# A two-layer hybrid block on one core: the triangular levels of both directions' last delta-rule chunks take an earlier rank in the order of steps

## The chip, the cores and the metric

The kernel runs on one core of a Trainium2 chip. The metric is the device time of one execution in microseconds (us); lower is better. The time before is the median of three executions, 2316.86 us.

## The reference, cut to what matters

Two layers work on one sequence of 1024 tokens with 1024 features, in float32. The first has a windowed attention beside a bidirectional gated delta rule, an output projection of both, and a feed-forward part; the second has three other branches and plays no role here. The delta rule in chunks, and what the first layer makes of it:

```python
def _chunk_gated_delta_rule(q, k, v, g, beta):
    ...
    t_mat = lax.linalg.triangular_solve(eye + a_mat, jnp.broadcast_to(eye, a_mat.shape),
                                        left_side=True, lower=True)
    w_c = jnp.einsum("bnhcs,bnhsd->bnhcd", t_mat, beta[..., None] * k * jnp.exp(gc)[..., None])
    u_c = jnp.einsum("bnhcs,bnhse->bnhce", t_mat, beta[..., None] * v)
    ...
    def step(state, xs):
        q_c, k_c, u, w, qk_c, gl = xs
        v_new = u - jnp.einsum("bhcd,bhde->bhce", w, state)
        o = jnp.einsum("bhcd,bhde->bhce", q_c, state) + jnp.einsum("bhcs,bhse->bhce", qk_c, v_new)
        state = state * jnp.exp(gl)[..., None, None] + jnp.einsum("bhcd,bhce->bhde", k_c, v_new)
        return state, o

def _gdn_mixer(qkv, z, a, b, conv_w, a_log, dt_bias, norm_w):
    ...
    o_fwd = _chunk_gated_delta_rule(q, k, v, g[:, :, 0], beta[:, :, 0])
    o_bwd = flip(_chunk_gated_delta_rule(flip(q), flip(k), flip(v), flip(g[:, :, 1]), flip(beta[:, :, 1])))
    o = _rmsnorm(o_fwd + o_bwd, norm_w) * jax.nn.silu(z.astype(f32).reshape(B, S, GDN_HEADS, GDN_HEAD_DIM))

def first_block(...):
    ...
    h = h + jnp.concatenate([attn, gdn], axis=-1) @ w_out[l]
```

## The kernel before, in words

Large products run in three passes on TensorE (PE). A float32 operand is split into a high part, rounded to the format fp32r, and the rest, its low part; per slab of 128 input features PE multiplies high by high (line 625), low weight by high (627) and high by low (629). So each 128 x 512 result tile, a job, takes 24 matmuls over 8 slabs. The stage of these jobs after the delta rule is the output projection, called P3 in the code: jobs 46 to 61. Jobs 46 and 47 cover half 1 of the sequence, 48 and 49 half 0. In each, slabs 0 to 3 read attention, slabs 4 to 7 the normed and gated delta-rule output.

**The delta rule.** It runs in chunks of 128 tokens, i = 0 to 7, in two directions, d = 0 (forwards) and d = 1 (backwards). The inverse of each chunk's triangular matrix is built from 32 x 32 blocks in two levels, l = 0 and 1. A level is a line of small steps: `la` (PE, lines 747 and 754) multiplies, `lp` (VectorE, called DVE; 1544 and 1547) copies the result to the tile P, `lb` (PE, 747 and 754) multiplies again, `lt` (DVE, 1558 and 1562) subtracts it from the tile T, `lx` (PE, 734) transposes T, and `ltt` (ScalarE, called ACT; 991) copies that to TT. The `la`, `lb` and `lx` steps of all chunks share a ring of three PSUM banks.

**The recurrence.** With the inverse at hand, a chunk does `cR` (PE, 702) and `cr` (DVE, 1570), `cT` (PE, 702) and `cn` (ACT, 991), `co` (PE, 800 and 801) and `cO` (DVE, 1584). All but the last chunk also do `crk` (ACT), `ckd` (PE, 702) and `cs` (DVE, 1592) for the state. Of these, `cR`, `cT`, `co` and `ckd` share a ring of two banks with `gs`. The norm of a finished chunk is `gsq` (ACT, 1181), the sum over features `gs` (PE, 811), `gr` (ACT, 995 and 997) and `gn` (DVE, 1602).

**Attention.** It runs over 8 blocks n of 128 queries: `aqk` (PE, 822), `am` (DVE, 1614), `as1` (DVE, 1621 to 1624), `ae` (ACT, 1193), `as2` (DVE, 1629 and 1631), `ap` (GpSimd, called POOL; 2128), and per key block s `atr` (PE, 830), `atc` (ACT, 991) and `apv` (PE, 840); the result is copied out by `ao` (DVE, 1642).

**The operands of P3.** For each half h and each slab j of attention, `ya` (a DMA issued by SP) loads the stored result, `yah` (ACT) makes the high part and `yal` (DVE, 1419) the low part. For the delta rule, `zl` loads the gate, `zm` (DVE, 1653) multiplies it in once the `gn` of four chunks are done (those of direction 0, `gn(0, 4..7)`, for half 1; those of direction 1 for half 0), `zh` (ACT) makes the high part and `zlo` (POOL, 2083) the low part. Half 0 reuses the buffers of half 1, so `ya(0, j)` waits for `yal(1, j)`. Result tiles are added by `evd` (DVE, 1668); `hac` (1408 and 1410) sums squares, and `ws` (1779 to 1792) prepares weights for a later stage.

**The order of the work.** A planner, `Plan.settle`, places every step once, ahead of time, on its engine. It keeps one clock for each engine, made from estimated durations, and at each point takes the step that can start first. Among steps of an engine that can start at the same moment, the one with the lower rank goes first:

```python
t = start(q, k)
c = (max(t, clock[q] + 40), info[k][3], seq[k], k)
...
clock[q] = t + r.ns
ends[k] = clock[q] + self.LAG[q]
```

The order that comes out is fixed in the program: each engine runs its steps in that order and waits on semaphores for those of others. Steps of the triangular levels have rank r = 4 + i/8, attention steps 1.5 + n/16, steps of the recurrence 2, norm sums 3 (2 for chunk 7), and the parts of the P3 jobs 9. The names to follow are `first_layer` (the loop over i and d, where `la` to `ltt` are added), `Plan.settle`, and the steps above.

Of the kernel before, what the change touches and what calls it, by code (L numbers as in the profile page):

```python
# [181 lines left out]
class Plan:  # L182
# [15 lines left out]
    def add(self, engine, name, *key, rank=5, ring=None, frees=None, behind=()):  # L198


        self.steps.append((engine, name, key, rank, ring, frees, behind))
# [2680 lines left out]
def first_layer(p, K):  # L2882
# [70 lines left out]
    for i in range(8):  # L2953
        for d in range(2):
            r = 4 + i / 8
            add("sp", "inv_in", d, i, rank=r)
            add("pool", "tex", d, i, rank=r - 1)
            add("sp", "gcl", d, i, rank=r)
            add("sp", "bel", d, i, rank=r)
            add("dve", "dd", d, i, rank=r)  # L2960
            add("act", "ebx", d, i, rank=r)
            add("pool", "sc", d, i, rank=r)
            add("dve", "a1", d, i, rank=r)
            before = [("lx", (d, i - 2, TOP))] if i >= 2 else [("lb", (0, 0, TOP)), ("lb", (1, 0, TOP))] if i else []
            add("sp", "kkl", d, i, rank=r)
            add("dve", "a2", d, i, rank=r)
            if i < 4:
                add("pe", "qk", d, i, rank=r, ring="prep", frees=[("qkc", (d, i))], behind=before)
                add("act", "qkc", d, i, rank=r)
                add("sp", "qk_out", d, i, rank=r)  # L2970
            else:
                add("sp", "qk_in", d, i, rank=r)
            add("dve", "qkm", d, i, rank=r)
            for l in range(len(LEVELS)):
                add("pe", "la", d, i, l, rank=r, ring="prep", frees=[("lp", (d, i, l))])
                add("dve", "lp", d, i, l, rank=r)
                add("pe", "lb", d, i, l, rank=r, ring="prep", frees=[("lt", (d, i, l))])
                add("dve", "lt", d, i, l, rank=r)
                add("pe", "lx", d, i, l, rank=r, ring="prep", frees=[("ltt", (d, i, l))])
                add("act", "ltt", d, i, l, rank=r)  # L2980
            if i:
                add("pe", "cR", d, i, rank=2, ring="chain", frees=[("cr", (d, i))], behind=[("co", (d, i - 1))])
                add("dve", "cr", d, i, rank=2)
            add("pe", "cT", d, i, rank=2, ring="chain", frees=[("cn", (d, i))] + ([("crk", (d, i))] if i < 7 else []))
            add("act", "cn", d, i, rank=2)
            add("pe", "co", d, i, rank=2, ring="chain", frees=[("cO", (d, i))], behind=[("co", (1 - d, 7 - i))] if i >= 4 else ())
            add("dve", "cO", d, i, rank=2)
            if i < 7:
                add("act", "crk", d, i, rank=2)
                add("pe", "ckd", d, i, rank=2, ring="chain", frees=[("cs", (d, i))], behind=[("co", (d, i))])  # L2990
                add("dve", "cs", d, i, rank=2)
            if i >= 4:
                r = 3 if i < 7 else 2
                add("act", "gsq", d, i, rank=r)
                add("pe", "gs", d, i, rank=r, ring="chain", frees=[("gr", (d, i))])
                add("act", "gr", d, i, rank=r)
                add("dve", "gn", d, i, rank=r)
    for g in range(2):
        add("sp", "abias", g)
    for n in range(8):  # L3000
        r = 1.5 + n / 16
# [207 lines left out]
def build(nc, A, out):  # L3209
# [12 lines left out]
    for b, j in enumerate(B.jobs):  # L3222
# [14 lines left out]
        else:  # L3237
            p.add("dve", "evd", b, rank=1)
    first_layer(p, K)
    second_layer(p, K)  # L3240

# [151 lines left out]
```

## Time and profile before

| | |
|---|---|
| time of three executions | 2317.94, 2316.86, 2314.18 us; median 2316.86 |
| the profiled execution | 2318.24 us, its span 2316.1 us |
| granted TensorE clock over the span | 0.991 of full speed |
| busy share of the span | PE 97%, DVE 69%, ACT 48%, POOL 45% |
| chain that ended last, by engine | PE 86%, DVE 7%, issue 3%, ACT 2%, DMA 2%, POOL 1% |

The busy shares are means over the whole span. A row of a timeline has the start, the time that the instructions of the row covered, engine, line, operation, shapes and count, and in brackets how long the engine had been idle ahead of it and what released it. Float32 matmuls that are not of the three-pass kind show as two records each, so a `gs` is x2, and an `apv`, which has two matmuls, x4. A fast record of the three-pass kind lasts 0.39 us, but the next one starts 0.23 us after it.

### The profile page before, as it was taken

Reading aid. Unit: us, or ns where it says so; the run is one execution under the profiler, and the core shown is the slowest. Engines: PE = TensorE matmul, PEld = TensorE weight load, DVE = VectorE, ACT = ScalarE, POOL = GpSimd, SP = SyncE. Lnnn points to the kernel's source line nnn. Section 1 sums busy time; section 2 is a strip of 40 time slices with the busy share of each in tenths; the row PEclk is TensorE's granted clock in tenths of the full one; section 3 lists DMA queues with packets and bytes.
Section 4 is the critical chain, followed back from the end, with each engine's and each line's share of the span. In section 5 each row is a group of like instructions: output and inputs, shape, how many; then the busy total and the mean of one; then the engine's idle time right before and its main releaser. Section 6 shows DMA issues by size and latency. Waiting matters only on the chain.

```text
span 2316.1 us, 31264 instructions
## 1 busy us (share of the span) xinstructions
PE 2256.4 (97%) x11389; PEld 1785.5 (77%) x11389; DVE 1606.4 (69%) x2217; ACT 1111.2 (48%) x2008; POOL 1034.5 (45%) x643
## 2 busy tenths in 40 slices
PE   9999979898989999999999999999999999999999
PEld 6778867666868888887887777777788888888886
DVE  7865767766497555589548779878978665546745
ACT  5654155765255555544445455555623332225653
POOL 2212244444147666656866311111123775546763
PEclk9999989999999999999999999999999999999999
DMA  4113453325224444755452301111033333338654
GB/s 158 45 38 98 131 169 97 107 86 190 91 83 173 169 154 150 272 187 175 154 171 79 132 28 46 46 46 46 28 105 123 132 132 112 114 126 291 195 172 147
DMA packets 153764, 289.43 MB, mean 125 GB/s; under 512 B 34915, under 2 KB 44387, under 8 KB 153612
## 3 DMA queue, kind: packets, MB, share of 16 engines
q1 hardware_dynamic: 153612, 287.44, 37.2%
q8 instruction: 91, 1.49, 0.3%
q14 instruction: 61, 0.50, 0.1%
HBM read 207.88 MB, written 79.51 MB: 124 GB/s over the span
## 4 chain that ended last, share of the span: by engine, by line
PE 86%; DVE 7%; issue 3%; ACT 2%; DMA 2%; POOL 1%; SPq 0%; DVEq 0%; ACTq 0%; POOLq 0%
PE bank L625 12%; PE bank L629 12%; PE bank L857 12%; PE bank L855 12%; PE bank L853 12%; PE bank L627 12%; PE bank L702 2%; PE bank L918 2%; PE bank L949 2%; PE bank L931 1%; ACT t L991 1%; DVE t L1419 1%; PE bank L840 1%; PE bank L830 1%; DVE t L1410 1%
## 5 line engine op out<-in xcount | busy, mean ns | idle before, releaser
L2083 POOL TENSOR_TENSOR t<-t,t 128x512 fp32r<-128x512 f32 (+1 forms) x494 | 814.7, 1661 | 1078.5 <-ACT t L991 1075.3
L991 ACT ACTIVATE t<-t 128x512 fp32r<-128x512 f32 (+1 forms) x689 | 448.9, 676 | 665.9 <-PE bank L857 252.9
L625 PE MATMUL bank<-t,t 128*128 128x512 f32 x1360 | 550.0, 404 | 0.6 <-ACT t L991 0.6
L629 PE MATMUL bank<-t,t 128*128 128x512 f32 x1360 | 532.7, 392 | 3.2 <-DVE t L1419 2.7
L627 PE MATMUL bank<-t,t 128*128 128x512 f32 x1360 | 531.1, 391 | 1.5 <-POOL t L2083 1.5
L853 PE MATMUL bank<-t,t 128*128 128x512 f32 x1316 | 513.8, 390 | 9.9 <-DVE t L1803 8.3
L857 PE MATMUL bank<-t,t 128*128 128x512 f32 x1316 | 513.0, 390 | 1.5 <-DVE t L1419 1.5
L855 PE MATMUL bank<-t,t 128*128 128x512 f32 x1316 | 512.8, 390 | 1.1 <-POOL t L2083 1.1
L625 PEld LDWEIGHTS bank<-t,t 128*128 128x128 f32 x1360 | 256.4, 189 | 64.0 <-issue 12.6
L629 PEld LDWEIGHTS bank<-t,t 128*128 128x128 f32 x1360 | 255.9, 188 | 61.1 <-DVE t L1419 3.5
L627 PEld LDWEIGHTS bank<-t,t 128*128 128x128 f32 x1360 | 256.5, 189 | 55.2 <-issue 4.5
L853 PEld LDWEIGHTS bank<-t,t 128*128 128x128 f32 x1316 | 247.4, 188 | 63.0 <-DVE t L1803 8.7
L855 PEld LDWEIGHTS bank<-t,t 128*128 128x128 f32 x1316 | 247.4, 188 | 54.1 <-POOL t L2083 2.1
L857 PEld LDWEIGHTS bank<-t,t 128*128 128x128 f32 x1316 | 247.3, 188 | 54.1 <-DVE t L1419 3.4
L1419 DVE TENSOR_TENSOR t<-t,t 128x512 fp32r<-128x512 f32 x192 | 181.9, 962 | 78.9 <-ACT t L991 78.3
L991 ACT ACTIVATE t<-bank 128x512 f32<-128x512 f32 (+2 forms) x255 | 142.9, 579 | 192.2 <-PE bank L931 45.0
L2033 DVE TENSOR_TENSOR t<-t,bank 128x512 f32<-128x512 f32 x105 | 70.2, 682 | 105.0 <-PE bank L857 104.6
L1959 DVE TENSOR_TENSOR_SCAN t<-t,t 128x512 f32<-128x512 f32 (+3 forms) x96 | 106.6, 1110 | 3.3
L1410 DVE TENSOR_TENSOR t<-t,t 128x512 f32<-128x512 f32 x55 | 74.9, 1362 | 30.2 <-ACT t L1367 16.3
L1437 DVE SCALAR_TENSOR_TENSOR t<-t,t,t 128x1024 f32<-128x1024 f32 x48 | 76.3, 1593 | 14.2 <-ACT t L991 12.9
L1719 DVE TENSOR_TENSOR t<-t,bank 128x512 f32<-128x512 f32 x48 | 32.9, 685 | 54.6 <-PE bank L629 44.4
L2102 POOL TENSOR_TENSOR t<-t,t 128x512 f32<-128x512 f32 x32 | 43.4, 1367 | 46.5 <-DVE t L1530 16.4
(250 smaller groups left out, 2684.2 us busy)
## 6 DMA issues: line engine op xcount, KB each, us to landing
t<-in_w SPq DMA_DIRECT2D x87, 512.0 KB, 3.5
hid_scr<-t SPq DMA_DIRECT2D x112, 256.0 KB, 2.2
t<-hid_scr SPq DMA_DIRECT2D x112, 256.0 KB, 2.7
t<-in_wf SPq DMA_DIRECT2D x80, 256.0 KB, 3.3
t<-in_wf SPq DMA_DIRECT2D x36, 512.0 KB, 4.4
g_scr<-t SPq DMA_DIRECT2D x36, 512.0 KB, 2.9
t<-g_scr SPq DMA_DIRECT2D x72, 256.0 KB, 3.9
t<-in_wo SPq DMA_DIRECT2D x24, 512.0 KB, 3.6
```

The lines of the kernel that those rows point to most:

```text
L625: e.matmul(ps[:, :], hi[:, w, :], XH[:, x, hs], start=k == 0, stop=False)
L627: e.matmul(ps[:, :], lo[:, w, :], XH[:, x, hs], start=False, stop=False)
L629: last = e.matmul(ps[:, :], hi[:, w, :], XL[:, x, hs], start=False, stop=k == j.nk - 1)
L853: e.matmul(ps, hi, XH, start=start, stop=False)
L855: e.matmul(ps, lo, XH, start=False, stop=False)
L857: return e.matmul(ps, hi, XL, start=False, stop=stop)
L991: return e.activation(out, in_, ACT.Copy, **kw)
L1410: tt(acc[:, :], acc[:, :], sq[:, :], ALU.add).then_inc(*tick(*name))
L1419: return tt(out, x, high.bitcast(F32), ALU.subtract)
L1437: stt(y[:, :] if j < 4 else dst, raw[:, j:j + S], w, y[:, :], ALU.mult, ALU.add).then_inc(*tick("cv", m))
L1959: e.tensor_tensor_scan(x[:, ::-1], one_c.broadcast_to([128, nk]), m_[:, ::-1], 0.0, ALU.mult, ALU.add).then_inc(*tick("ss", a, i, p_))
L2083: return e.tensor_tensor(out, x, high.bitcast(F32), ALU.subtract)
```

## The change

In the loop over chunks, the rank of `la`, `lp`, `lb`, `lt`, `lx` and `ltt` is set to 2 - d for the last chunk, i = 7, in place of 4 + 7/8: so 2 in direction 0 and 1 in direction 1. The steps added ahead of it in the loop keep their rank; those of the recurrence have 2 in any case.

```diff
@@ -2971,6 +2971,8 @@
             else:
                 add("sp", "qk_in", d, i, rank=r)
             add("dve", "qkm", d, i, rank=r)
+            if i == 7:
+                r = 2 - d
             for l in range(len(LEVELS)):
                 add("pe", "la", d, i, l, rank=r, ring="prep", frees=[("lp", (d, i, l))])
                 add("dve", "lp", d, i, l, rank=r)
```

No instruction is added or taken away. All engines keep their counts; what moves is their order between the attention of block 6 and the first jobs of P3. Three places follow, rows before and rows in the changed program.

On DVE, around the state update of chunk 6, direction 0 (`cs(0,6)`, line 1592). The rows at 1614 are `am` of block 7, those from 1621 to 1624 are `as1(7)`. Before:

```order
L1592 SCALAR_TENSOR_TENSOR t_117<-t_117,t_84,bank 128x128 x4
L1614 ISA t_148,t_156<-bank,t_144 128x256
L1614 ISA t_156 128x1
L1614 ISA t_149,t_156<-bank,t_145 128x256
L1614 ISA t_156 128x1
L1621 TENSOR_TENSOR t_156<-t_156,t_80 128x2x4
L1623 TENSOR_SCALAR t_156<-t_156 128x2x4
L1624 TENSOR_TENSOR t_156<-t_80,t_156 128x2x4
```

The changed program at the same place, with `cO(0,6)` (line 1584) on top:

```order
L1584 TENSOR_TENSOR t_150<-t_150,bank 128x512
L1614 ISA t_148,t_156<-bank,t_144 128x256
L1614 ISA t_156 128x1
L1614 ISA t_149,t_156<-bank,t_145 128x256
L1614 ISA t_156 128x1
L1621 TENSOR_TENSOR t_156<-t_156,t_80 128x2x4
L1623 TENSOR_SCALAR t_156<-t_156 128x2x4
L1624 TENSOR_TENSOR t_156<-t_80,t_156 128x2x4
L1592 SCALAR_TENSOR_TENSOR t_117<-t_117,t_84,bank 128x128 x4
```

The state update now stands behind `as1(7)`.

On PE, the end of the recurrence. 811 is a norm sum, 754 with t_126 is `lb(1,7,1)`, 840 is `apv(7,1)`, 734 is `lx(1,7,1)`, 702 with t_126 is `cT(1,7)`, and 800 and 801 are `co(1,7)`. Before:

```order
L811 MATMUL bank<-t_119,t_49 128x512
L811 MATMUL bank<-t_157,t_49 128x512
L754 MATMUL bank<-t_120,t_126 64x64 x4
L840 MATMUL bank<-t_151,t_73 64x512
L840 MATMUL bank<-t_152,t_73 64x512
L734 MATMUL bank<-t_49,t_122 128x128 x4
L702 MATMUL bank<-t_134,t_126 128x128 x4
L800 MATMUL bank<-t_132,t_133 128x128
L801 MATMUL bank<-t_128,t_134 128x128
```

In the changed program, from `cR(1,7)` on:

```order
L702 MATMUL bank<-t_133,t_69 128x128 x4
L811 MATMUL bank<-t_157,t_49 128x512
L702 MATMUL bank<-t_134,t_126 128x128 x4
L840 MATMUL bank<-t_151,t_73 64x512
L840 MATMUL bank<-t_152,t_73 64x512
L811 MATMUL bank<-t_119,t_49 128x512
L800 MATMUL bank<-t_132,t_133 128x128
L801 MATMUL bank<-t_128,t_134 128x128
```

The level's steps are gone from here; they stand ahead of `atr(6,0)`. Behind `co`, before, came the last norm sum `gs(1,7)` and then job 46. In the changed program the first 18 matmuls of job 46 come first (slabs 0 to 5), then `gs(1,7)`, then the last six.

On DVE, the operands of P3. 1419 is `yal`, 1653 `zm`, 1668 `evd`, 1602 here `gn(1,7)`, and 1657 and 1658 are one small step, `gg`. Before:

```order
L1657 TENSOR_TENSOR t_173<-t_49 128x8
L1658 TENSOR_TENSOR t_174<-t_49 128x8
L1419 TENSOR_TENSOR t_59<-t_159,t_58 128x512 x2
L1602 SCALAR_TENSOR_TENSOR t_150<-t_150,t_49,t_119 128x512
L1419 TENSOR_TENSOR t_59<-t_159,t_58 128x512
L1653 TENSOR_TENSOR t_160<-t_150,t_160 128x512
L1653 TENSOR_TENSOR t_161<-t_150,t_161 128x512
L1419 TENSOR_TENSOR t_59<-t_159,t_58 128x512
L1668 TENSOR_TENSOR t_158<-t_158,bank 128x512
```

In the changed program:

```order
L1657 TENSOR_TENSOR t_173<-t_49 128x8
L1658 TENSOR_TENSOR t_174<-t_49 128x8
L1668 TENSOR_TENSOR t_158<-t_158,bank 128x512
L1602 SCALAR_TENSOR_TENSOR t_150<-t_150,t_49,t_119 128x512
L1408 COPY t_165<-t_170 128x512
L1653 TENSOR_TENSOR t_160<-t_150,t_160 128x512
L1419 TENSOR_TENSOR t_59<-t_159,t_58 128x512
L1653 TENSOR_TENSOR t_161<-t_150,t_161 128x512
L1668 TENSOR_TENSOR t_158<-t_158,bank 128x512
L1419 TENSOR_TENSOR t_59<-t_159,t_58 128x512
```

`evd(46)`, which waits for the whole of job 46, now stands ahead of `gn(1,7)`, and `evd(47)` ahead of `yal(0,1)`. Further down, `yal(0,3)` has moved ahead of three of the four `ws` steps. On POOL, `wlo(25)`, the low part of a weight tile, has moved ahead of `zlo(1,3)`. On SP the four loads of the residual (`hx`) have moved behind `ya(1, 0..3)`.

## Rows read from the trace of the kernel before

**Rows 1.** By stretch: us, busy of PE, PEld, DVE, ACT, POOL, then clock, DMA, GB/s
```profile
515.00:548.00 33.00, 26.86 (x163) 19.25 (x163) 16.52 (x27) 22.95 (x51) 16.14 (x9) 0.90 0.62 218
548.00:563.00 15.00, 15.00 (x60) 12.06 (x58) 13.54 (x17) 7.98 (x17) 7.43 (x5) 0.89 0.42 135
```
**Rows 2.** Who PE waited for, 480 to 600 us: total, times, longest
```profile
PE bank L629 <- DVE t L1419: 2.7, 1, 2.7
...
PE bank L734 <- DVE t L1562: 0.7, 1, 0.7
```
**Rows 3.** Timeline of PE, from apv(6,0) to the jobs of P3
```profile
517.24 1.53 PE L840 MATMUL bank<-t,t 128*64 128x512 f32 x4 [1.29 <-ACT t L991]
...
529.93 0.39 PE L800 MATMUL bank<-t,t 128*128 128x128 f32 x2
...
531.82 1.08 PE L840 MATMUL bank<-t,t 128*64 128x512 f32 x4
...
535.57 0.68 PE L754 MATMUL bank<-t,t 64*64 64x64 f32 x8
...
539.35 1.16 PE L702 MATMUL bank<-t,t 128*128 128x128 f32 x8 [1.51 <-ACT t L991]
541.35 0.57 PE L800 MATMUL bank<-t,t 128*128 128x128 f32 x2 [0.84 <-ACT t L991]
...
544.28 0.63 PE L801 MATMUL bank<-t,t 128*128 128x128 f32 x2
547.11 1.13 PE L811 MATMUL bank<-t,t 128*128 128x512 f32 x2 [2.19 <-ACT t L1181]
547.67 0.79 PE L625 MATMUL bank<-t,t 128*128 128x512 f32 x1
```
**Rows 4.** The same timeline, where P3 stops for its operands
```profile
551.56 0.54 PE L625 MATMUL bank<-t,t 128*128 128x512 f32 x1
...
565.86 0.80 PE L629 MATMUL bank<-t,t 128*128 128x512 f32 x1 [2.66 <-DVE t L1419]
566.45 0.63 PE L625 MATMUL bank<-t,t 128*128 128x512 f32 x1
```
**Rows 5.** Timeline of POOL
```profile
506.21 5.46 POOL L2128 TENSOR_TENSOR t<-t,t 128x1536 f32<-128x1536 f32 x2 [11.69 <-DVE t L1631]
...
540.28 9.42 POOL L2083 TENSOR_TENSOR t<-t,t 128x512 fp32r<-128x512 f32 x5 [2.49 <-ACT t L991]
```
**Rows 6.** Timeline of DVE, attention of blocks 6 and 7
```profile
498.69 0.17 DVE L1621 TENSOR_TENSOR t<-t,t 128x8 f32<-128x8 f32 x1
...
507.69 1.12 DVE L1592 SCALAR_TENSOR_TENSOR t<-t,t,bank 128x128 f32<-128x128 f32 x4 [0.30 <-PE bank L702]
...
509.54 2.15 DVE L1621 TENSOR_TENSOR t<-t,t 128x8 f32<-128x8 f32 x1
```
**Rows 7.** Timeline of DVE, the operands of P3
```profile
538.27 0.68 DVE L1642 COPY t<-bank 128x512 f32<-128x512 f32 x1
...
544.04 1.75 DVE L1419 TENSOR_TENSOR t<-t,t 128x512 fp32r<-128x512 f32 x1
...
549.73 1.28 DVE L1419 TENSOR_TENSOR t<-t,t 128x512 fp32r<-128x512 f32 x2
550.94 0.74 DVE L1602 SCALAR_TENSOR_TENSOR t<-t,t,t 128x512 f32<-128x512 f32 x1
...
555.31 0.69 DVE L1668 TENSOR_TENSOR t<-t,bank 128x512 f32<-128x512 f32 x1 [1.22 <-PE bank L629]
...
565.13 0.68 DVE L1419 TENSOR_TENSOR t<-t,t 128x512 fp32r<-128x512 f32 x1
```
**Rows 8.** Timeline of ACT: exponentials of block 7, then atc(6,0) and cn(1,6)
```profile
511.99 0.51 ACT L1193 ACTIVATE t<-t,t 128x256 f32<-128x256 f32 x1 [1.26 <-DVE t L1624]
...
516.14 1.54 ACT L991 ACTIVATE t<-bank 128x512 f32<-128x512 f32 x3
```
**Rows 9.** Who PE waited for in the whole span: its longest later wait
```profile
PE bank L853 <- DVE t L1803: 8.3, 1, 8.3
```

## The prediction
> **What bounds the kernel now.** I read the page first: PE is busy for 97% of the span and holds 86% of the chain that ended last, so a change of order can only win or lose where PE waits, or runs at the lower of its two clock levels (1.2 and 2.4 GHz; a granted clock of 0.5 and of 1.0). The reader should then look for such places near the edit. The view by stretch shows them: 26.86 us busy of 33 and a granted clock of 0.90 from 515 to 548 us, and 0.89 up to 563 us [rows 1]. The view of waits names them, and the timeline places them. At the end of the recurrence PE waits 1.51 us for ACT ahead of `cT(1,7)`, 0.84 us ahead of `co(1,7)` and 2.19 us ahead of the last norm sum `gs(1,7)`; later it waits 2.66 us for `yal(0,3)`, in the middle of job 48 [rows 2 to 4]. Lastly I read DVE and POOL beside each other from 538 us on, since they make the operands that PE is given there [rows 5, 7].
>
> **What the change does, part by part.** The work is the same, so I follow the new order with the durations of the rows, and ask where PE stands against before when `yal(0,3)` comes. From there on the order is the same but for small things.
>
> *1. Up to apv(6,0).* PE gets five small steps of chunk 7, direction 0, ahead of the last scores `aqk(6,3)`, and loses one, each about 0.6 us (one took 0.68 with its tail, [rows 3]): +2.4 us, of which I let short waits there cover 0.4. The rest of the attention block hangs on these scores: `as1`, `ae`, `as2`, then `ap(6)` on POOL, which took 5.46 us for two instructions and ended at 511.67 [rows 5]. I put its new end at 513.4. This matters because of what DVE does at that time. The first instruction of `as1` took 0.17 us at 498.69, with POOL at rest, and 2.15 us at 509.54, which is just until POOL ended; the update at 1592, which reads a bank, took its usual 1.12 us beside the same POOL work [rows 5, 6]. So DVE instructions whose operands all lie in SBUF wait for POOL. Before, `cs(0,6)` stood ahead of `as1(7)` and was done at 508.8. Now it is behind: as1 is let go at 513.4, and 0.4 + 1.1 us later, at 514.9, `cR(0,7)` may start, for which PE is ready at about 513. **A new wait of about 1.8 us**, which takes the place of the two (0.7 for 1562 and 1.29 us, [rows 2, 3]) that PE has shortly ahead of 517.24. From as1's release to `apv(6,0)` it was 5.25 us before (511.99 to 517.24, [rows 3, 8]), which gives 518.9. Over PE (three steps of 0.5 to 1.0 us, part of them at the low clock, then `atc`, two of the three copies that took 1.54 us, [rows 8]) it is 518.3 to 519.9. I take 519.4, +2.2 us.
>
> *2. From there to P3.* Before: 547.67 - 517.24 = 30.4 us [rows 3]. Out go the second level of (1,7), now done (1.7), the three waits (4.5), the norm sum (0.6 here), and the low clock of `co(1,7)` (1.6: from 541.35 to the end at 544.91 it took 3.56 us, the same step for (0,7) 1.89 from 529.93 to 531.82). In come `cT(1,6)`, which now stands later (0.9), and a wait for `cr(1,7)` (0.5), since only one norm sum of 0.9 lies between `cR(1,7)` and `cT(1,7)`. That leaves 23.4 us [rows 3], so **P3 could start at 542.8 instead of 547.7, 4.9 us sooner**.
>
> *3. The operands of half 1.* They are not there yet. `ao(7)` follows `apv(7,1)`, which now has `gs(1,6)` and `co(1,7)`, 2.7 us, between itself and P3: 540.3 against 538.27 [rows 7], +2.0. Behind it comes DVE's list, alternating with POOL. Four `zlo` and a `wlo` took 9.42 us, and a `yal` 1.75 us where a turn of POOL (1.15) came first, 0.64 where none did [rows 5, 7]. From `ao(7)` to the end of `yal(1,3)` it was 12.7 us (538.27 to 551.01). Now `gn(1,6)` and `gg` are behind it, but their turns of POOL stay in the stretch, since `wlo(25)` has moved ahead too, so I take off 0.9 only: 552.1. Against 551.0 that is +1.1, where PE had been promised -4.9. PE used slab 3 at 551.56 [rows 4], so **the whole lead is lost in front of slabs 0 to 3**. Each wait also keeps the clock low.
>
> *4. Job 46.* After `yal(1,3)` come seven products, at 0.43 us each because PE has just idled (as in [rows 4] at 565.86: 0.59 and 0.43 to the next), 3.0; then `gs(1,7)`, 1.1; then six products, 1.5. End: 557.7. Before, `evd(46)` started at 555.31 [rows 7]: +2.4. The Trainium skill's page "TensorE: Matmul & The Clock Gate" (section "HAM oscillation — how this bites in real kernels") warns that pauses in front of matmuls bring the low clock back, here again and again; the trace agrees so far that all three long waits of [rows 3, 4] are followed by products at half speed. Were the clock to stay high, the seven products would take 1.6 and the sum below would be +3.6.
>
> *5. The operands of half 0.* This is the step that decides. `gn(1,7)` ran at 550.94 [rows 7], before job 46 was done. Now it stands behind `evd(46)`, so it starts at 558.4, and with it all `zm(0, j)`. `evd(47)` stands ahead of `yal(0,1)` and needs job 47, 24 products at 0.228 = 5.5 us later, 563.2. Behind it are eight DVE instructions up to the end of `yal(0,3)` at 0.62 each, 5.0, and two to three turns of POOL at 1.15: 570.5 to 571.6. Before it was 565.81. **+4.7 to +5.8; I take +5.0**, nearer to two turns, since two of the four `zlo` have time to run while DVE waits for `evd(47)`. The three `ws` that no longer stand ahead (2.8 us) are already in this.
>
> *6. After that.* The low clock behind the stop (1.4 us, seven products) comes again. `hx` is loaded some 10 us later, but its late half belongs to jobs from the 50s on. A wait of 8.3 us for DVE stands far behind, at 678 us [rows 9]; DVE's chain ahead of it starts with the norm after P3, so I let the shift pass through.
>
> The Trainium skill's page "SBUF — State Buffer" (section "SBUF: two separate sides") says that GpSimd and DVE instructions with two SBUF inputs take one port pair as an exclusive lock, for a whole instruction, whoever starts first. The trace agrees: 2.15 us for an 8-column instruction, and none of it for a bank operand. By the page's rule points 1, 3 and 5 stand with their turns of POOL; were it to share bandwidth instead, the result would be the second rival's.
>
> **The sum.** +5.0 us on the profiled execution, 2318.24, gives 2323.2. That one is 1.4 us over the median, so against the median of 2316.86 I forecast **2321.9 us**. The bounds of this case: with the smallest values `yal(1,3)` ends at 551.1, job 46 runs on at the high clock (3.9 us to its end), and one turn of POOL follows: 551.1 + 3.9 + 5.6 + 5.0 + 1.15 = 566.8, +0.9. With the largest it ends at 553.1, all of job 46's rest runs at the low clock (6.9 us), and three turns follow: 574.0, +8.2.
>
> **The rivals.** *Faster.* The operands keep up, as P3's early start suggests. Then the waits of 1.5, 0.8 and 2.2 us are gone, and P3 runs from 542.8. This needs DVE to be through `yal(0,3)` before job 48's slab 3, at 542.8 + 5.5 x 2 + 3 = 557. That is the point from which it decides, and it wins 4.9 + 2.7 + 1.4 (low clock) = 9 us: 2307.9. Against it speaks that DVE was busy for 13.54 of the 15 us up to 563 [rows 1], and the new list is not shorter. Half of it, about 2312, would need POOL to stay out of the way. Chance 0.12.
>
> *A wash.* The gain at the start and the loss at the end come out even. This is what the same sums give without turns of POOL: `cs(0,6)` is not held (-1.8), `yal(1,3)` is there at about 548 and `yal(0,3)` at 563 to 566. It also comes out if the shift is swallowed by the 8.3 us wait [rows 9], should that hang on something that does not move. -3 to +0.9: 2314 to 2317.8. Chance 0.26.
>
> *Slower by starvation* is my own case. Chance 0.62; its upper part, over +4.6 us, 0.46, the lower part 0.16. Speaking for it: both `evd` in DVE's queue now tie the next half's operands to PE's progress, which was not so before.
>
> **How the numbers follow.** No change that I can measure means within 0.2%, 4.6 us, of 2316.86. Faster: 0.12. Within: 0.16 + 0.25 = 0.41. Slower: 0.46 + 0.01 = 0.47. The range runs from the lower end of the wash to the largest bound of my own case: 2314.0 to 2325.0. It leaves out most of the faster case and some thin ends. My own case alone is 2317.8 to 2325.0.
>
> **What would show it.** In the changed kernel's profile: `as1(7)`'s 1621 lasting 1.5 us or more and ending with POOL, directly ahead of a late 1592; a PE wait of 1 to 2 us at 702 near 514 us; no wait of PE for ACT at `cT(1,7)` and `gs(1,7)`; the first P3 product near 543 us, followed by waits of PE for 1419 adding up to 5 us or more before 553 us; `gn(1,7)` near 558 us, behind 1668; and PE stopped again for 1419 in job 48, until about 571 us. I am wrong if `yal(0,3)` ends before 566 us, if the first P3 product does not come sooner, or if PE's stop in front of the pair stage (853, 8.3 us) is shorter by as much as P3 is late.

## The result and the profile after

The changed kernel takes 2323.39 us (median of 20 runs, 2318.93 to 2327.72), the kernel before 2319.56 us (20 runs). The ratio is 1.0020, 95% interval 1.0013 to 1.0028: **slower by 4.6 us, 3.0 to 6.5**. (The ratio is not quite that of the two medians, which are 3.8 us apart; all differences in time below go by ratios.) The forecast was 2321.9 us, +5.0 against the 2316.86 us known then. Its profiled execution took 2320.31 us, with a span of 2318.3.

The two traces can't be laid over each other from zero. Between 316 and 350 us, where both programs are alike, the granted clock was 0.80 in the one of before and 0.90 in the other, and 3.0 of the 3.1 us by which they are apart ahead of the change arise there. So I count from the first instruction of `as1(5)`, the last mark ahead of the change: 456.24 us before, 453.10 after. The timeline of DVE in the kernel before, there and at `evd(49)`, the end of the second pair of jobs:

```profile
456.24 1.19 DVE L1621 TENSOR_TENSOR t<-t,t 128x8 f32<-128x8 f32 x1
...
576.01 0.69 DVE L1668 TENSOR_TENSOR t<-t,bank 128x512 f32<-128x512 f32 x1 [1.55 <-PE bank L629]
```

The same timeline in the changed kernel, with the places of [rows 6, 7]:

```profile
453.10 1.19 DVE L1621 TENSOR_TENSOR t<-t,t 128x8 f32<-128x8 f32 x1
...
508.38 1.96 DVE L1621 TENSOR_TENSOR t<-t,t 128x8 f32<-128x8 f32 x1
...
510.54 1.11 DVE L1592 SCALAR_TENSOR_TENSOR t<-t,t,bank 128x128 f32<-128x128 f32 x4
...
534.70 0.68 DVE L1642 COPY t<-bank 128x512 f32<-128x512 f32 x1
...
544.38 2.83 DVE L1419 TENSOR_TENSOR t<-t,t 128x512 fp32r<-128x512 f32 x1
...
553.35 0.69 DVE L1668 TENSOR_TENSOR t<-t,bank 128x512 f32<-128x512 f32 x1 [4.29 <-PE bank L629]
553.96 0.75 DVE L1602 SCALAR_TENSOR_TENSOR t<-t,t,t 128x512 f32<-128x512 f32 x1
...
558.79 0.69 DVE L1668 TENSOR_TENSOR t<-t,bank 128x512 f32<-128x512 f32 x1 [1.81 <-PE bank L629]
...
564.28 1.74 DVE L1419 TENSOR_TENSOR t<-t,t 128x512 fp32r<-128x512 f32 x1
...
577.51 0.69 DVE L1668 TENSOR_TENSOR t<-t,bank 128x512 f32<-128x512 f32 x1 [1.60 <-PE bank L629]
```

From `as1(5)` to `evd(49)` it was 119.8 us and is 124.4, so this stretch alone has 4.6 us; behind it another 0.7 came up in this pair of traces (1740.1 and 1740.8 us to the end). The rows show how: DVE now stands idle 4.29 us ahead of `evd(46)` and 1.81 ahead of `evd(47)`, with `gn(1,7)` (553.96) and `yal(0,3)` (564.28) queued behind them. The 1621 of 1.96 us ends at 510.34, with POOL's two instructions of `ap(6)`, as in [rows 5, 6]:

```profile
504.87 5.45 POOL L2128 TENSOR_TENSOR t<-t,t 128x1536 f32<-128x1536 f32 x2 [12.33 <-DVE t L1631]
```

Who PE waited for from 480 to 610 us, in place of [rows 2]:

```profile
PE bank L629 <- DVE t L1419: 9.1, 6, 3.0
PE bank L840 <- ACT t L991: 1.7, 1, 1.7
PE bank L702 <- DVE t L1592: 1.2, 1, 1.2
```

And the timeline of PE, for [rows 3, 4]:

```profile
511.70 1.16 PE L702 MATMUL bank<-t,t 128*128 128x128 f32 x8 [1.24 <-DVE t L1592]
...
515.90 1.08 PE L840 MATMUL bank<-t,t 128*64 128x512 f32 x4 [1.73 <-ACT t L991]
...
537.74 0.47 PE L625 MATMUL bank<-t,t 128*128 128x512 f32 x1 [0.27 <-ACT t L991]
...
542.23 0.80 PE L629 MATMUL bank<-t,t 128*128 128x512 f32 x1 [2.29 <-DVE t L1419]
...
547.27 0.79 PE L629 MATMUL bank<-t,t 128*128 128x512 f32 x1 [2.12 <-DVE t L1419]
...
550.42 1.51 PE L811 MATMUL bank<-t,t 128*128 128x512 f32 x2
...
566.08 0.80 PE L629 MATMUL bank<-t,t 128*128 128x512 f32 x1 [2.99 <-DVE t L1419]
...
571.36 0.63 PE L629 MATMUL bank<-t,t 128*128 128x512 f32 x1
```

P3 starts at 537.74, by the common count 6.8 us sooner than in [rows 3]. Then it starves three times in job 46 (2.29 and 2.12 us are the long ones) and three times in job 48 (2.99 the last). Behind that last stop 13 products run 0.43 us apart (566.08 to 571.36); before, seven did. The view by stretch:

```profile
515.00:548.00 33.00, 26.65 (x157) 18.43 (x158) 18.81 (x26) 21.07 (x40) 18.23 (x9) 0.90 0.63 224
548.00:563.00 15.00, 13.73 (x50) 9.80 (x48) 8.76 (x16) 8.18 (x17) 3.69 (x4) 0.89 0.37 139
```

These are not the stretches of [rows 1], since the traces are 3.1 us apart. The same view of the kernel before, for the same part of the count:

```profile
518.14:551.14 33.00, 28.45 (x165) 21.02 (x164) 19.04 (x28) 22.14 (x45) 16.45 (x9) 0.86 0.68 239
551.14:566.14 15.00, 12.34 (x53) 9.95 (x52) 13.20 (x17) 5.65 (x11) 5.72 (x4) 0.96 0.42 140
```

Up to the end of the first stretch PE is less busy than before, 26.65 against 28.45 us; in the second one it is more busy, but at a lower clock, and the long stop of job 48, inside it before, now comes behind it. So busy shares don't show the loss here; the single waits do.

The wait of 8.3 us for 1803 in front of the pair stage is unchanged, so the shift passed through it.

### The profile page after: what moved, and what is told of

It is laid out like the page before. It is cut to its first block, busy times and chain, and to the rows that moved or that the text cites. A ratio compares the mean times of both kernels' runs of the same rounds, so it can differ in the third digit from the quotient of the medians.

```text
span 2318.3 us, 31262 instructions
## 1 busy us (share of the span) xinstructions
PE 2255.3 (97%) x11389; PEld 1783.9 (77%) x11389; DVE 1597.4 (69%) x2217; ACT 1112.6 (48%) x2008; POOL 1034.5 (45%) x643
## 4 chain that ended last, share of the span: by engine, by line
PE 88%; DVE 6%; ACT 2%; issue 2%; DMA 1%; POOL 0%; SPq 0%; DVEq 0%; ACTq 0%; POOLq 0%
PE bank L625 13%; PE bank L629 13%; PE bank L627 13%; PE bank L857 12%; PE bank L853 12%; PE bank L855 12%; PE bank L702 2%; PE bank L918 2%; PE bank L949 2%; PE bank L931 1%; ACT t L991 1%; DVE t L1419 1%; PE bank L840 1%; PE bank L830 1%; PE bank L822 1%
```

## Experiments

The theory is that of the prediction: the operands of P3 decide, above all the late `gn(1,7)` and the two `evd` ahead of half 0's low parts. Rival A: the early steps on PE, or the new wait at `cR(0,7)`, carry the loss. Rival B: DVE's and POOL's work binds, in whatever order.

All kernels but one move steps by hand, after the planner has made its lists. `ahead(q, x, *steps)` takes the steps out of engine q's list and puts them in front of x, `behind` puts them behind it; nothing else in the program changes:

```diff
-        self.order = order
+        self.order = moved(order)
```

Each was timed against the kernel before. "Count" is the time from `as1(5)` to `evd(49)` in the kernel's own trace.

| kernel | from | ratio to before, 95% | us to before | count |
|---|---|---|---|---|
| before | | | | 119.8 |
| changed | | 1.0020 (1.0013 to 1.0028) | +4.6 | 124.4 |
| e1_cs | changed | 1.0035 (1.0022 to 1.0048) | +8.1 | 125.9 |
| e2_ops | changed | 1.0009 (0.9999 to 1.0018) | +2.1 | 119.9 |
| e3_before_ops | before | 0.9986 (0.9976 to 0.9996) | -3.2 | 115.5 |
| e4_tail | changed | 1.0042 (1.0029 to 1.0055) | +9.7 | 125.9 |
| e5_tail | changed | 1.0021 (1.0010 to 1.0031) | +4.9 | 121.9 |
| e6_tail_ops | changed | 0.9995 (0.9986 to 1.0004) | -1.2 | 116.3 |
| e7_atc | changed | 0.9991 (0.9983 to 1.0000) | -2.1 | 116.3 |
| e8_gn | changed | 1.0028 (1.0017 to 1.0039) | +6.5 | 125.8 |
| e9_gsq | changed | 0.9988 (0.9979 to 0.9997) | -2.8 | 114.6 |
| e10_before_atc | before | 0.9988 (0.9978 to 0.9998) | -2.8 | 113.2 |
| e11_d0 | before | 1.0032 (1.0022 to 1.0042) | +7.4 | 123.0 |
| e12_best | before | 0.9970 (0.9957 to 0.9982) | -7.0 | 113.8 |

Set against the 119.8 of the kernel before, the counts differ from the times by up to 4.2 us. A count is one execution, and what is left of the span behind `evd(49)` was between 1739.9 and 1743.9 us in these traces, though the order there is the same. The interval of a ratio is 2 to 3 us to either side, and a difference between two rows of the table carries both, about 3 us. So of the steps between variants, the times alone show only the large ones (e6 against the changed kernel, against e5, and e2 against e3; e6 against e2 and e12 against e10 barely); the others rest on the counts and on single places in the traces.

**e1_cs.** The new wait at `cR(0,7)` taken away.

```diff
+    ahead("dve", ("as1", (7,)), ("cs", (0, 6)))
```

> The changed kernel with cs(0,6) ahead of as1(7) on DVE again. Theory 1 (the operands of P3 decide; the wait at cR(0,7) is only their smaller feeder): the PE wait at 702 near 511.7 us (1.24) is gone or under 0.4, apv(6,0) comes 1.0 to 1.5 us sooner, so does ao(7), and the time falls by 1.0 to 1.5 us against the changed kernel, +3 to +4 against the kernel before. Rival A (the new wait at cR(0,7) behind as1(7) is what costs): the time falls by 4 to 5 us, to the kernel before. Rival B (the operands are bound by DVE and POOL work, whatever PE does): ao(7) comes sooner, but nothing behind it, 0.

No theory had it: it was no faster than the changed kernel, rather slower, 8.1 us to 4.6 in time (on five executions, and the intervals overlap) and 125.9 to 124.4 in the count. The timeline of its PE and of its ACT, the exponentials of block 7 and `atc(6,0)`:

```profile
512.75 1.16 PE L702 MATMUL bank<-t,t 128*128 128x128 f32 x8
...
518.25 1.08 PE L840 MATMUL bank<-t,t 128*64 128x512 f32 x4 [3.03 <-ACT t L991]
519.26 1.56 PE L830 MATMUL bank<-t,t 128*128 128x128 f32 x8
520.61 3.16 PE L702 MATMUL bank<-t,t 128*128 128x128 f32 x16
```

```profile
513.00 0.51 ACT L1193 ACTIVATE t<-t,t 128x256 f32<-128x256 f32 x1 [1.34 <-DVE t L1624]
...
517.14 1.05 ACT L991 ACTIVATE t<-bank 128x512 f32<-128x512 f32 x2
```

The wait at 702 is gone, and `apv(6,0)` comes no sooner: counted from `as1(5)` it is at 62.9 us, in the changed kernel at 62.8. The path there doesn't touch `cs`. It is `ap(6)` on POOL, which holds the first instruction of `as1(7)` to its end, then eight exponentials, then `atc(6,0)` behind them on ACT. The 1.24 us that PE waited at `cR` were only part of that wait; now it is 3.03 us in one piece, and the matmuls behind it run at the lower level (16 matmuls of 702 in 3.16 us; in the changed kernel 1.95). That puts `ao(7)` 1.7 us later. Rival A falls for the wait at `cR(0,7)`. The Trainium skill's page "TensorE: Matmul & The Clock Gate" (section "HAM oscillation — how this bites in real kernels") warns that pauses of PE bring the low clock back. In these traces the length of one pause doesn't tell whether it does: behind 3.03 us here it came, behind 1.24 and 1.73 us in the changed kernel it did not, and in the kernel before it came behind 0.69 and 1.29 us ([rows 3], `apv(6,0)` at 1.53 us).

**e2_ops and e3_before_ops.** The same edit on both kernels: the second tie, `evd(47)`, and the weights' steps off the path to `yal(0,3)`.

```diff
+    behind("dve", ("yal", (0, 3)), ("evd", (47,)), ("hac", (3, 1, 1)), ("ws", (0, 3)), ("ws", (0, 2)), ("ws", (0, 1)), ("ws", (0, 4)))
```

> The changed kernel with evd(47), hac(3,1,1) and ws(0,3) moved on DVE from ahead of yal(0,1), yal(0,2), yal(0,3) to behind yal(0,3). Theory 1 (evd(47), which needs all of job 47, holds the low parts of half 0): yal(0,3) ends near 561 to 562.5 in place of 566.0, the stop of PE in job 48 (0.25 + 1.01 + 2.99) shrinks below 1.5, the low clock behind it (13 products, 2.6 us) does not come: 3 to 5.5 us faster than the changed kernel, -1 to +1.5 against the kernel before. Rival A (the wait at cR(0,7)): nothing, 0. Rival B (DVE's and POOL's work bind, not the order): yal(0,3) ends no more than 1.2 us sooner (the two instructions taken out ahead of it), 1 us faster at most.

> The kernel before with the same edit: evd(47), hac(3,1,1) and all four ws behind yal(0,3). The changed kernel's early part is absent. Theory 1: in the kernel before, yal(0,3) stands behind five instructions for later work (3.9 us) though PE stops 2.66 us for it; now it ends near 562, the stop is under 0.5 and the low clock behind it is gone: 3 to 4 us faster than the kernel before. Rival B (work, not order): 0 to 1 us faster. If the load ya(0,3) is late (it waits for yal(1,3), about 551): PE still stops, 1 us or so.

Both came as the theory has it, e2_ops a little short in time (2.5 us for 3 to 5.5, which by time alone is within the noise). In e2_ops, DVE around `yal(0,3)` (563.74; 109.1 us behind `as1(5)` at its end, in the changed kernel 112.9), and PE in job 48 behind it:

```profile
563.74 0.68 DVE L1419 TENSOR_TENSOR t<-t,t 128x512 fp32r<-128x512 f32 x1
564.34 0.68 DVE L1668 TENSOR_TENSOR t<-t,bank 128x512 f32<-128x512 f32 x1
```

```profile
563.27 0.50 PE L629 MATMUL bank<-t,t 128*128 128x512 f32 x1 [0.45 <-DVE t L1419]
...
564.47 0.50 PE L629 MATMUL bank<-t,t 128*128 128x512 f32 x1 [0.24 <-DVE t L1419]
...
567.61 0.50 PE L629 MATMUL bank<-t,t 128*128 128x512 f32 x1 [0.62 <-POOL t L2083]
...
569.29 0.50 PE L629 MATMUL bank<-t,t 128*128 128x512 f32 x1 [0.72 <-POOL t L2083]
```

The stop of 2.99 us is 0.24, and no product of job 48 runs at half speed. The count falls by 4.5, the time by 2.5 us. In e3_before_ops the wait for 1419 is gone altogether, and the kernel is 3.2 us faster than the one it came from. That refutes rival B, and it also says what the step can't do: **the edit wins about the same in both kernels (4.5 and 4.3 in the count)**. So `evd(47)` and `hac(3,1,1)` ahead of `yal(0,1)`, and one `ws` further down, cost in the changed kernel what `evd(47)` and five instructions for later work ahead of `yal(0,3)` cost in the other. It is not the difference between them; with it gone from both, 4.5 us remain (119.9 against 115.5).

**e4_tail and e5_tail.** The changed kernel up to `ao(7)`, then the lists of the kernel before. `DVE_BEFORE` stands for DVE's steps of before from `zm(1,0)` to `yal(0,3)`. The last two lines are in e4_tail only.

```diff
+    ahead("pe", ("mp", (46, 0)), ("gs", (1, 7)))
+    behind("dve", ("ao", (7,)), *DVE_BEFORE)
+    behind("act", ("yah", (0, 3)), ("hsq", (3, 1, 0)))
+    behind("pool", ("zlo", (1, 3)), ("wlo", (25,)))
+    ahead("sp", ("aout", (6,)), ("hx", (2, 1)), ("hx", (3, 1)), ("hx", (2, 0)), ("hx", (3, 0)))
+    ahead("sp", ("ya", (1, 0)), ("wload", (25,)))
```

> The changed kernel up to ao(7), and from there the order of the kernel before: gs(1,7) ahead of job 46 on PE, DVE's list from ao(7) to yal(0,3), the place of hsq(3,1,0) on ACT, wlo(25) behind zlo(1,3) on POOL, hx ahead of aout(6) on SP. Theory 1: ao(7) starts near 534.7 as in the changed kernel's trace (counted from the same clock stretches) and the tail takes as long as before (538.27 to 565.81, 27.5 us), so the stop ends near 562.2 in place of 566.1: 3 to 4.5 us faster than the changed kernel, about equal to the kernel before (0 to +1.5). Rival A (the early part carries the loss): stays at +4 or more against the kernel before. Rival B: between, because the list of DVE is as long either way: +2 to +4.

> e4_tail without its two edits on SP: the changed kernel up to ao(7), from there the kernel before's order on PE (gs(1,7) ahead of job 46), DVE, ACT (hsq(3,1,0)) and POOL. In e4_tail, hx ahead of aout(6) waited for cR(1,7) and held the stored attention 9 us. Counted from as1(5) in each trace, evd(49) came after 119.8 us in the kernel before and 124.4 in the changed one. Theory 1 (the loss is made in the tail: gn(1,7) is 6.1 us later there because gs(1,7) stands behind 18 products and gn(1,7) behind evd(46), and evd(47) is ahead of yal(0,1)): with ao(7) 81.6 us behind as1(5) (before 82.0) and a tail as before, 119.0 to 120: within 1 us of the kernel before, 4 to 5 faster than the changed one. Rival A (the early steps on PE, 1.9 us, are what is lost): +2 or more against the kernel before.

Both missed. The timeline of the DMA queue of SP in e4_tail, and DVE at `ao(7)`:

```profile
533.50 1.93 SPq L2192 DMA_DIRECT2D t<-in_xT  x4
535.48 0.61 SPq L2192 DMA_DIRECT2D attn_scr<-t  x1
```

```profile
543.26 0.69 DVE L1642 COPY t<-bank 128x512 f32<-128x512 f32 x1 [6.26 <-DMA attn_scr<-t]
```

`hx(2)` and `hx(3)` wait for `cR(1,7)`, which stands later in the changed kernel, and `aout(6)` waited behind them on SP; `ao(7)` must wait for `aout(6)` (line 1636). In the changed kernel `hx` stands behind `aout(6)`, where this wait holds nothing up. I had costed that move at nothing, rightly as it stood and wrongly as a thing that may be undone.

e5_tail has `ao(7)` where it should be (81.8 us). What holds it is the norm. Who PE waited for, and the instruction of ACT that ended the first of these waits:

```profile
PE bank L811 <- ACT t L1181: 6.9, 1, 6.9
PE bank L629 <- DVE t L1419: 3.6, 1, 3.6
```

```profile
545.76 0.61 ACT L1181 ACTIVATE t<-t 128x512 f32<-128x512 f32 x1
```

`gsq(1,7)` stands on ACT behind eight copies for P3 and one for a weight tile, the last five of which ran from 542.71 to 545.8. In the kernel before it is ahead of two of them, `yah(1,2)` and `yah(1,3)`; I had left it where the changed kernel has it, so the tail was not the one of before after all. And `cO(1,7)`, which `gsq(1,7)` needs, stands on DVE behind `gn(1,6)` and `yal(1,0)`, as in the kernel before, where it was PE that came late. Its count is 2.5 us better than the changed kernel's, its time is not. The transplant proves little either way.

**e6_tail_ops and e8_gn.** e6 is e5_tail with the edit of e2. e8 takes the first tie alone out of the changed kernel:

```diff
+    ahead("pe", ("mp", (46, 1)), ("gs", (1, 7)))
+    ahead("dve", ("yal", (1, 2)), ("gn", (1, 6)))
+    ahead("dve", ("evd", (46,)), ("gn", (1, 7)))
```

> e5_tail and evd(47), hac(3,1,1), four ws behind yal(0,3). Theory 1: both gains add up, 115 us from as1(5) to evd(49): 4 to 5 us faster than the kernel before, as e3_before_ops (so the early part of the change is worth 0.4 us at most). Rival: if half 0's operands were held by the early part too, only as e2_ops.

> The changed kernel with the norm of chunk 7 alone put early: gn(1,6) ahead of yal(1,2) on DVE, gs(1,7) behind the first nine products of job 46 on PE, gn(1,7) ahead of evd(46). evd(47) stays ahead of yal(0,1). Theory 1 (two ties in series): gn(1,7) 4 to 6 us sooner, but yal(0,3) ends where it did or up to 1 us sooner, since evd(47) still needs job 47: 0 to 1.5 us faster than the changed kernel. Rival (the late gn(1,7) alone carries the loss): 4 us faster.

e8 gains nothing (+6.5 against +4.6 us, 125.8 against 124.4 in the count), and neither expectation holds. `gn(1,7)` runs 2.9 us ahead of `evd(46)`, but counted from `as1(5)` it is only 1.8 us sooner than in the changed kernel, and job 46 is later: `yal(1,3)` ends 0.8 us later behind `gn(1,6)`, PE waits 1.0 us for the early `gs(1,7)`, and `evd(46)` and `evd(47)` come 1.7 us later. From `evd(47)` to the end of `yal(0,3)`, at 566.86, it takes 7.2 us, just as in the changed kernel:

```profile
551.31 0.75 DVE L1602 SCALAR_TENSOR_TENSOR t<-t,t,t 128x512 f32<-128x512 f32 x1 [3.97 <-ACT t L997]
...
559.63 0.69 DVE L1668 TENSOR_TENSOR t<-t,bank 128x512 f32<-128x512 f32 x1 [1.83 <-PE bank L629]
...
565.12 1.74 DVE L1419 TENSOR_TENSOR t<-t,t 128x512 fp32r<-128x512 f32 x1
```

e6, with the tail in the order of before and the edit of e2, is 5.8 us faster than the changed kernel, and 3.3 faster than e2 (3.6 in the count). That is less than was expected of it: 1.2 us faster than the kernel before where 4 to 5 were forecast, 116.3 in the count for 115.

**The ties lie in series: `yal(0,3)` follows `evd(47)` by 7.2 us with `gn(1,7)` sooner or not, and with `evd(47)` out of the way the order of the rest is worth 3.6 us in the count.** The places fit that. In e2 PE still stops four times in job 48, 0.45 and 0.24 us for `yal`, 0.62 and 0.72 for `zlo`; in e6, with `gn(1,7)` 6.5 us sooner, not once. But e6 moves DVE's whole list, `gs(1,7)`, `wlo(25)` and an `hsq` together, and e8, which moves the norm nearly alone, slows job 46 down; so that the late norm carries the 3.6 us is argued, not shown.

With the edit of e2 in all three, the 4.5 us between changed and before split into 3.6 for the order of the tail (e2 to e6) and 0.9 for the rest (e6 to e3; 2.0 by the ratios, with 3 to either side). The rest holds the early steps on PE and the late `gsq(1,7)` of e6, so it bounds rival A for the early steps, by the count.

**e7_atc and e9_gsq.** e7 is e6 with the two places at `apv(6,0)` that e1 pointed to; e9 adds the two for `gsq(1,7)`.

```diff
+    ahead("dve", ("as1", (7,)), ("cs", (0, 6)))
+    behind("act", ("ae", (0, 7)), ("atc", (0, 6, 0)), ("atc", (1, 6, 0)))
```

```diff
+    ahead("dve", ("yal", (1, 0)), ("cO", (1, 7)))
+    ahead("act", ("yah", (1, 2)), ("gsq", (1, 7)))
```

> e6_tail_ops, and cs(0,6) ahead of as1(7) on DVE, and on ACT atc(0,6,0) and atc(1,6,0) between ae(0,7) and ae(1,7) instead of behind both. In e1_cs the wait at cR(0,7) went (1.2 us) and came back ahead of apv(6,0) (1.7 grew to 3.03), because atc(6,0) stood behind eight exponentials of block 7 on ACT (4.1 us), which wait for POOL by way of as1(7). Theory: that chain bounds the place, so apv(6,0) comes 1.5 to 2 us sooner, ao(7) and the operands too: 1.5 to 2 us faster than e6_tail_ops, no low clock near 519 us. Rival: the copies only push the exponentials, POOL's ap(7) and atr(7,0) back by 1 us: 0.

> e7_atc, with cO(1,7) ahead of yal(1,0) on DVE and gsq(1,7) ahead of yah(1,2) on ACT. In e5 to e7 PE waited 6.3 to 6.9 us ahead of gs(1,7) for gsq(1,7), which stood on ACT behind six copies for P3, and job 46 began 92 us after as1(5) though half 1's low parts were done at 91.0 to 92.4. Theory (this wait is now the last on the path): the wait falls to 2 to 3.5 us, P3 begins at 87 to 89, job 46 ends 3 to 5 us sooner, yal(0,3) 1 to 3 sooner, evd(49) at 112.5 to 115 in place of 116.3: 1.5 to 3.5 us faster than e7_atc. Rival (half 0's low parts then stop PE in job 48): a new wait for 1419 of 1 to 2 us and half of the gain only.

In e7 `apv(6,0)` comes 1.8 us sooner than in e6 and `ao(7)` 0.3: a new wait of 1.3 us at 702 for ACT's `gr(0,6)`, pushed back by the copies, took most of it. The count is that of e6, as its rival said, if by another step. In e9 the wait for `gsq(1,7)` is 2.3 in place of 6.8 us and the count 1.7 better; the time is not measurably so (0.9991 and 0.9988). Its views of waits, where half 0's operands now stop PE a little, as its rival said:

```profile
PE bank L811 <- ACT t L1181: 2.3, 1, 2.3
PE bank L629 <- DVE t L1419: 2.0, 3, 1.0
PE bank L629 <- POOL t L2083: 1.3, 2, 0.7
```

**e11_d0.** One part of the change alone: rank 2 for direction 0, direction 1 as before, with all that the planner makes of it.

```diff
+            if i == 7 and d == 0:
+                r = 2
```

> The rank changed for direction 0 alone (2), direction 1 stays at 4 + 7/8. The order of the tail then keeps gs(1,7) ahead of job 46 and gn(1,7) ahead of evd(46), as before; yal(0,3) stays behind ws. Theory 1 (the tail's order is what costs): within 2 us of the kernel before. Rival A (the early PE steps ahead of block 6's scores cost 2 us and are not given back): +2 to +4.

+7.4 us: missed, and for neither reason.

```profile
PE bank L734 <- DVE t L1558: 5.8, 1, 5.8
PE bank L702 <- ACT t L991: 3.0, 2, 2.9
```

Now `lt(1,7,1)` stands on DVE behind three `zm`, a `yal` and `gn(1,6)`, and `lx(1,7,1)`, `cT(1,7)` and `co(1,7)` wait for it. The planner's tail is a new one each time, so this kernel says nothing on the early steps alone.

**e10_before_atc and e12_best.** The findings put onto the kernel before, without the change: e3's edit, ACT's copies between the exponentials, and in e12 two more places on DVE.

```diff
+    behind("act", ("ae", (0, 7)), ("atc", (0, 6, 0)), ("atc", (1, 6, 0)), ("cn", (1, 6)))
+    ahead("dve", ("yal", (1, 0)), ("cO", (1, 7)))
+    behind("dve", ("yal", (1, 3)), ("gg", ()))
```

> e3_before_ops (the kernel before's ranks), and on ACT atc(0,6,0), atc(1,6,0) and cn(1,6) between ae(0,7) and ae(1,7). Theory: PE's wait of 1.29 us at apv(6,0) goes, ao(7) comes 1 to 1.5 us sooner, and everything to the end of job 49 with it: 1 to 1.5 us faster than e3_before_ops, more if the low clock near 515 us stays away (1.5 us). Rival (as in e7_atc, where 1.2 us were won at apv(6,0) and only 0.3 at ao(7)): 0 to 0.5.

> e10_before_atc, with cO(1,7) ahead of yal(1,0) and gg behind yal(1,3) on DVE: the version with the fewest waits so far, on the kernel before's ranks. In e10, gs(1,7) waited 3.70 us for gsq(1,7), which waited for cO(1,7) behind a yal, and gg (8 columns) held DVE 2.32 us behind a turn of POOL, ahead of yal(1,2). Theory: gs(1,7) 1 to 1.7 us sooner, yal(1,3) up to 1.2 sooner, job 49's end 0.5 to 1.5 sooner: 0.5 to 1.5 us faster than e10_before_atc and 4 to 7 us in the trace against the kernel before. Rival (POOL's turn only moves to the next instruction): yal(1,3) where it was, 0 to 0.5.

e10 has `ao(7)` 2.0 us sooner than e3 and the count 2.2 lower, more than expected; the time doesn't show it (0.9988 and 0.9986). e12_best is the fastest of all, 2310.82 us, 7.0 us (4.2 to 10.0) below the kernel before. Its wait for `gsq(1,7)` is 1.4 us in place of 3.7. `yal(1,3)` came not a moment sooner (92.8 us in both): without `gg` the turn of POOL fell on the `yal` themselves, as its rival said. How much of e12's lead over e10 (4.2 us by the ratios) is the edit, I leave open: the count has it 0.6 us behind, with more of P3's start at the lower clock level.

## Why the prediction was right

The forecast was +5.0 us, the ratio says +4.6, and starvation was the case with most of the chance. (The absolute forecast is 1.5 us low: the kernel before came out 2.7 us higher in the 20 executions than in the first three, and the medians are 3.8 us apart.) Of its steps, all counted from `as1(5)`:

1. *Up to `apv(6,0)`*: +2.2 forecast, +1.8 measured. `as1(7)`'s 1621 took 1.96 us and ended with POOL's multiplication at 510.3, as the Trainium skill's page "SBUF — State Buffer" (section "SBUF: two separate sides") would have it. The steps ahead of the scores cost 1.9 (`as1(6)` 42.45 to 44.35 us). The 5.25 us of the prediction run from the first exponential, 0.3 us behind as1's release; its 518.9 has them in. The wait at `cR(0,7)` came (1.24) but, as e1 showed, it is not on the path; the chain by way of ACT gives the same number.
2. *P3's start*: -4.9 forecast, -6.8 measured. The three waits went as said. The term that was mis-sized is the low clock behind `apv(6,0)`, which I had kept: in the kernel before that step (1.53 us in [rows 3]), the `atr` and the first two records at 800 and 801 behind it took 4.0 us, in the changed kernel, where the step takes 1.08, the same work would be 2.4.
3. *Half 1's operands*: `ao(7)` +2.0 forecast, -0.4 measured, `yal(1,3)` +1.1 and -0.7, for the most part for the same reason; from the one to the other it took 12.5 us, 11.8 forecast. That the lead is lost in front of slabs 0 to 3 held: PE waits 4.8 us there.
4. *`evd(46)`*: +2.4 forecast, +1.2 measured.
5. *Half 0's operands*: `gn(1,7)` +7.5 forecast, +6.2 measured; the end of `yal(0,3)` +5.0 and +3.4. From `evd(47)` on it took 7.2 us with two turns of POOL, the lower end of the forecast.
6. *Afterwards*: nothing forecast, +1.3 measured: the stop brought 13 slow products in place of seven.

So the sum is right by two errors of 1.6 and 1.3 us against each other. That the sum came so near is luck in part; that the lead turns into a loss, and where, is not.

"This is the step that decides" was half right. Both ties cost time in the changed kernel: `evd(47)` out of the way and the tail in another order win 5.8 us together. But the one I put most of the sum on, `evd(47)`, has its like in the kernel before (the `ws` and `hac` steps that stand with it ahead of `yal(0,3)`), whose removal there wins as much; I counted it only as 2.8 us gained. What tells the two kernels apart is the order of the tail, 3.6 of 4.5 us in the counts with that edit on both sides, and within it most likely the late norm of chunk 7. Without that edit the same transplant (e5, with its late `gsq`) won 2.5 us in the count and nothing in the time.

## What to carry to other kernels

Before a queue entry that needs the whole of a product (`evd`), ask what stands behind it that the next product needs; in the three kernels where it was put later, together with the small steps for later work, it was worth 2.5 to 6 us (4.3 to 5.6 in the count), and no wait of PE for its bank showed up. When steps are moved, by a planner or by hand, look at what now stands ahead of them in a queue: three such places here (`hx` ahead of `aout`, `gsq` behind copies, `lt` behind `zm`) each went with a wait of 5.8 to 6.9 us. And a wait that ends in something further back isn't won by removing its front part; it only becomes one longer wait.

## What was not expected of the hardware

Two short waits of PE, 1.24 and 1.73 us, left the clock alone (granted 1.00 from 515 to 522 us), and one of 3.03 us in their place was followed by matmuls at the lower level; but so were two of only 0.69 and 1.29 us in the kernel before (0.50 from 518 to 521 us). What decides between them, these traces don't show. An instruction on 8 columns (`gg`) took 2.32 us beside POOL and 0.15 without it, but moving it away did not speed up those behind it: the turn of POOL fell on the next one (four `yal` in 5.21 us). And executions differ by the granted clock long before the change, in a part where all the programs are alike (0.75 to 0.90 between 316 and 350 us), which was 3 us between the two profiled ones of before and after; in a program of 2317 us that is two thirds of the effect measured.
